# Scan levels on 32x32 quarters, idle products on TensorE, and scattered expert rows in a hybrid encoder layer

## The reference

```
h  = rms_norm(x) * (1 + scale1) + shift1          # scale, shift, gate from silu(c) @ w_ada
p  = h @ w_in                                     # p_rwkv, p_mla, p_gate
y_a = rwkv7_mixer(p_rwkv)                         # 8 heads of 64, forward and backward
y_b = mla_mixer(p_mla)                            # 8 heads, softmax attention
x  = x + gate1 * ((g_a * y_a + g_b * y_b) @ w_out)
x  = x + gate2 * hier_moe(rms_norm(x) * (1 + scale2) + shift2)
```

```
sa    = state @ (-kk_t)
state = state * w_t + outer(sa, kk_t * a_t) + outer(v_t, k_t)
y_t   = state @ r_t
```

## Time and profile before

| | us |
|---|---|
| median of 3 runs | 2738.7 |
| lowest and highest run | 2731.55, 2768.6 |
| the profiled execution | 2732.23 |
| its span in the trace | 2730.4 |

### The profile page before, as it was taken

One profiled execution on the slowest core, in us unless ns is written; L12 is line 12 of the kernel. 1 busy time (PEld: TensorE's weight loads), 2 busy tenths in 40 slices (PEclk: granted clock), 3 DMA queues, 4 the chain that ended last, 5 costly groups with the idle time before them and its releaser, 6 DMA issues. The chain is left out here.

```text
span 2730.4 us, 52710 instructions
## 1 busy us (share of the span) xinstructions
PE 2433.9 (89%) x22191; PEld 1962.5 (72%) x22191; DVE 1595.7 (58%) x2165; ACT 1062.4 (39%) x1865; POOL 677.5 (25%) x498
## 2 busy tenths in 40 slices
PE   5799999999994999999979889998997994999990
PEld 2488887788884999999869756665876883666760
DVE  4444469966652354555445566666886445677756
ACT  5311133344441345445445455554122220555542
POOL 1122245545432345434213320001200000000004
PEclk8899999999995699999869989999998995999995
DMA  8422234443324132332043391103755123999977
GB/s 360 172 77 78 78 106 146 142 158 133 140 110 156 45 88 69 88 92 65 19 133 109 101 326 51 33 24 113 245 164 195 69 70 140 400 422 418 414 298 300
DMA packets 178735, 433.31 MB, mean 159 GB/s; under 512 B 38298, under 2 KB 90298, under 8 KB 160834
## 3 DMA queue, kind: packets, MB, share of 16 engines
q1 hardware_dynamic: 148548, 323.10, 34.1%
q0 software_dynamic: 15840, 57.54, 5.5%
q10 hardware_dynamic: 14112, 49.29, 4.5%
HBM read 307.15 MB, written 122.73 MB: 157 GB/s over the span
## 5 line engine op out<-in xcount | busy, mean ns | idle before, releaser
L99 PE MATMUL ps_in<-h_t_low,w_in_high 128*128 128x512 f32 x960 | 379.6, 395 | 10.5 <-POOL w_in_low L490 10.5
L100 PE MATMUL ps_in<-h_t_high,w_in_low 128*128 128x512 f32 x960 | 374.6, 390 | 0.0
L101 PE MATMUL ps_in<-h_t_high,w_in_high 128*128 128x512 f32 x960 | 374.6, 390 | 0.0
L99 PEld LDWEIGHTS ps_in<-h_t_low,w_in_high 128*128 128x128 f32 x960 | 180.7, 188 | 53.0 <-POOL w_in_low L490 11.5
L1191 POOL TENSOR_TENSOR wkv_levels<-wkv_nt,level_mask 128x1024 f32<-128x1024 f32 x60 | 140.1, 2353 | 274.5 <-ACT wkv_nt L1140 274.5
L101 PEld LDWEIGHTS ps_in<-h_t_high,w_in_high 128*128 128x128 f32 x960 | 180.6, 188 | 38.2
L100 PEld LDWEIGHTS ps_in<-h_t_high,w_in_low 128*128 128x128 f32 x960 | 180.8, 188 | 36.0
L2963 DVE TENSOR_TENSOR w_low<-w_now,w_high 128x2048 fp32r<-128x2048 f32 x64 | 146.7, 2292 | 39.3 <-ACT w_high L2800 39.3
L598 ACT COPY p_row<-ps_in 128x512 f32<-128x512 f32 x72 | 42.3, 588 | 304.5 <-PE ps_in L101 278.9
L2670 POOL DMA_INDIRECT xb<-h,row_ids x34 | 32.9, 967 | 511.1 <-PE ps_xy L2715 285.4
L488 POOL CAST w_in_high<-w_in_tile 128x1024 fp32r<-128x1024 f32 x40 | 46.6, 1164 | 335.8 <-PE ps_in L101 299.5
(11 more groups left out here) (383 smaller groups left out, 5788.9 us busy)
## 6 DMA issues: line engine op xcount, KB each, us to landing
w_now<-in_w SPq DMA_DIRECT2D x68, 1024.0 KB, 9.5
w_tile<-in_w SPq DMA_DIRECT2D x34, 1024.0 KB, 9.4
w_ada_tile<-in_w_ada SPq DMA_DIRECT2D x12, 2048.0 KB, 12.3
wkv_in<-wkv_out SPq DMA_DIRECT2D x24, 1024.0 KB, 3.9
w_in_tile<-in_w_in SPq DMA_DIRECT2D x40, 512.0 KB, 3.6
yb<-yb_tile ACTq DMA_DIRECT2D x34, 512.0 KB, 9.3
yb<-att_zeros POOLq DMA_DIRECT2D x32, 512.0 KB, 18.2
p_t<-p_mixed ACTq DMA_DIRECT2D x24, 512.0 KB, 2.7
```

The costliest lines, as they stand in the source:

```text
L99: nc.tensor.matmul(out, w[0], x[1], start=start, stop=False)
L100: nc.tensor.matmul(out, w[1], x[0], start=False, stop=False)
L101: return nc.tensor.matmul(out, w[0], x[0], start=False, stop=stop)
```

## The change

- In the scan, `nt`, `lev` and `z` hold only the diagonal 32x32 blocks. A level product becomes 64 calls with a 32x32 stationary tile, over four quarters, where it was 32 calls of 64x64. The masks, POOL's multiplications and ACT's copy of z are half as wide (one copy for z), `first_inverse` is one POOL instruction where it was two, `keep_nt` is four copies of 32 partitions where it was two of 64. `half_product` reads `lbm` and not `nt`.
- `keep_busy` issues products that nobody reads: 20 at the start of the scan, 24 before the first level of j = -1, 3 behind each of nine steps of j = -1, 12 at the start of `finish_and_merge`, and in routing 10 behind the counts and 6 behind the product of the lists.
- The product of the lists now gives the place of each row (token + 1536 k + 1; 0 where there is no token). DVE makes two lists from it, `row_from` and `row_to`, with indices beyond the bounds for rows without a token; six DVE instructions where there was one. Gathers and stores skip such rows. `xb` is cleared once.
- The results are stored by POOL as a scatter to `yb`, now laid out as two result rows per token, in place of ACT's direct stores. The zeroing of `yb` is dropped.
- `combine` reads `yb` with one direct transfer per tile, issued by SP; the two loads of `gate2` move from SP's queue to POOL's.

The diff, cut to its core:

```diff
+def keep_busy(nc, consts, out, n):
+    for _ in range(n):
+        nc.tensor.matmul(out, consts["ident"][:], consts["p_end"][:].rearrange("p d f n -> p (d f n)"), start=True, stop=True)
...
-        nt = s.sb("wkv_nt", [P, 2, 2 * H, CH])
-        lev = s.sb("wkv_levels", [P, LEVELS, 2 * H, CH])
+        nt = s.sb("wkv_nt", [P, 2, 2 * H, BLK])
+        lev = s.sb("wkv_levels", [P, LEVELS, 2 * H, BLK])
...
+        quads = [quad(c, b) for c in range(2) for b in range(2)]
...
                 for h in range(2 * H):
-                    for c in range(2):
-                        mm = nc.tensor.matmul(LV[half(c), 0, h], lev[half(c), l, h], x[half(c), i % 2, h], start=True, stop=True)
+                    for a in quads:
+                        mm = nc.tensor.matmul(LV[a, 0, h], lev[a, l, h], x[a, i % 2, h], start=True, stop=True)
...
-                        mm = nc.tensor.matmul(LV[half(c), 1, h], z[half(c), h], xt[half(c), i % 2, h], start=True, stop=True)
+                        mm = nc.tensor.matmul(LV[a, 1, h], z[a, h], xt[a, i % 2, h], start=True, stop=True)
...
+            def idle(j, n):
+                if j < 0:
+                    keep_busy(nc, consts, W[:].rearrange("p h t -> p (h t)")[:, 0:2 * RF * TOK // CH], n)
+            idle(-2, 20)
             for j in range(-2, N):
                 if inner:
+                    idle(j, 24)
                     level_z(j + 1, 1)
+                    idle(j, 3)
...
-                nc.scalar.mul(z[:, :, 0:BLK], LV[:, 0], blk[:, 0:1])
-                nc.scalar.mul(z[:, :, BLK:CH], LV[:, 0], blk[:, 1:2]).then_inc(m["z_kept"], 1)
+                nc.scalar.copy(z[:], LV[:, 0]).then_inc(m["z_kept"], 1)
...
-            for n in range(TOK * TOP // MB, BLOCKS):
-                pool.dma_start(dram["yb"][n], zeros[:]).then_inc(zeros_stored, 16)
...
+            keep_busy(nc, consts, ps_b[:].rearrange("p f t -> p (f t)")[:, 0:2 * RF * TOK // CH], 12)
             for u in range(len(units)):
...
+            def gather(b, offset):
+                pool.indirect_dma_start(out=xb[:, b], out_offset=None, in_=dram["h2"], in_offset=rows_at(offset),
+                                        bounds_check=TOK - 1, oob_is_err=False).then_inc(x_in[b], 16)
+            def scatter(b, offset):
+                pool.indirect_dma_start(out=dram["yb"], out_offset=rows_at(offset), in_=yb[:, b], in_offset=None,
+                                        bounds_check=TOP * TOK - 1, oob_is_err=False).then_inc(stored[b], 16)
+            def store(t):
+                pool.wait_ge(m["y_act"], t + 1)
+                pool.wait_ge(m["y_dve"], t + 1)
+                scatter(t % 2, row_to[:, t:t + 1])
+            for t in range(STATIC + 4):
+                if t < STATIC:
+                    if t >= 2:
+                        pool.wait_ge(m["turned"], t - 1)
+                    gather(t % 2, row_from[:, t:t + 1])
+                if t >= 4:
+                    store(t - 4)
...
+            keep_busy(10)
             for k in range(TOP):
...
+            keep_busy(6)
...
-                act.dma_start(dram["yb"][bass.ds(at, 1)].rearrange("a p d -> p (a d)"), yb[:, b]).then_inc(stored[b], 16)
...
+            def load(t):
+                sp.dma_start(picked[:, b], yb[P * t:P * t + P]).then_inc(gathered[b], 16)
```

More of the change, by code:

```diff
@@ L2597, in route_and_experts @@
         ended, block_e = view("ended", OVER, E), view("block_e", OVER + 1)
-        rank, expert, shift, full, row, blk, dest = (view(n, KT) for n in ("rank", "expert", "shift", "full", "row", "blk", "dest"))
+        rank, expert, shift, full, row, blk = (view(n, KT) for n in ("rank", "expert", "shift", "full", "row", "blk"))
         full_c = view("full_all", KT, TT - 1)
+        place, place_part = (view(n, BLOCKS) for n in ("place", "place_part"))
         early.close()
@@ L2666, in _ @@
         def _(pool):
+            nc.gpsimd.memset(xb[:], 0.0).then_inc(m["cleared"], 1)
+            pool.wait_ge(m["cleared"], 1)
             pool.wait_ge(m["ids"], 1)
-            def gather(t, b, offset):
-                pool.indirect_dma_start(out=xb[:, b], out_offset=None, in_=dram["h2"],
-                                        in_offset=bass.IndirectOffsetOnAxis(ap=offset.bitcast(U32), axis=0)).then_inc(x_in[b], 16)
-            for t in range(STATIC):
-                if t >= 2:
-                    pool.wait_ge(m["turned"], t - 1)
-                gather(t, t % 2, ids[:, t:t + 1])
+            rows_at = lambda offset: bass.IndirectOffsetOnAxis(ap=offset.bitcast(U32), axis=0)
+            def gather(b, offset):
[15 more added lines that the diff above has]
+                    store(t - 4)
             def body(i, ts):
@@ L2696, in _, with keep_busy @@
             nc.tensor.matmul(counts, consts["ones"][:], sums[:, T], start=True, stop=True).then_inc(m["counted"], 1)
+            def keep_busy(n):
+                for _ in range(n):
+                    nc.tensor.matmul(ps_xy[0][:, 0, 0:NTABLES], consts["ident"][:], consts["tables"][:], start=True, stop=True)
+            keep_busy(10)
             for k in range(TOP):
@@ L3005, in _, with combine @@
             over_pairs(dve, body)
-def combine(nc, dram, consts, x1, weight, slot):
+def combine(nc, dram, consts, x1, weight):
     BUF = 4
@@ L3020, in combine @@
         block = ctx.enter_context(nc.Block())
-        yb = dram["yb"].rearrange("b p d -> (b p) d")
+        yb = dram["yb"].rearrange("(k n) d -> n k d", k=TOP)
         @block.sync
         def _(sp):
-            for q in range(2):
-                row = (GATE2 * 2 + q) * DF
-                sp.dma_start(gate2[:, q], dram["mod_rows"][row:row + DF, :].rearrange("f p -> (f p)").partition_broadcast(P)).then_inc(consts_in, 16)
+            def load(t):
+                b = t % BUF
+                if t >= BUF:
+                    sp.wait_ge(done[b], t // BUF)
+                sp.dma_start(picked[:, b], yb[P * t:P * t + P]).then_inc(gathered[b], 16)
+            for t in range(BUF):
+                load(t)
             for t in range(TT):
@@ L3036, in _ @@
         def _(pool):
-            for t in range(TT):
-                b = t % BUF
-                if t >= BUF:
-                    pool.wait_ge(done[b], t // BUF)
-                for k in range(TOP):
-                    pool.indirect_dma_start(out=picked[:, b, k], out_offset=None, in_=yb,
-                                            in_offset=bass.IndirectOffsetOnAxis(ap=slot[:, k, t:t + 1], axis=0)).then_inc(gathered[b], 16)
+            for q in range(2):
+                row = (GATE2 * 2 + q) * DF
+                pool.dma_start(gate2[:, q], dram["mod_rows"][row:row + DF, :].rearrange("f p -> (f p)").partition_broadcast(P)).then_inc(consts_in, 16)
         @block.scalar
@@ L3099, in encoder @@
         weight = s.sb("weight", [P, TOP, TT])
-        slot = s.sb("slot", [P, TOP, TT], U32)
-        route_and_experts(nc, dram, consts, logits, weight, slot)
-        combine(nc, dram, consts, merged, weight, slot)
+        route_and_experts(nc, dram, consts, logits, weight)
+        combine(nc, dram, consts, merged, weight)
 INTERNAL = {
@@ L3116 @@
     "h2": (TOK, D),
-    "yb": (BLOCKS, MB, D),
+    "yb": (TOP * TOK, D),
 }
@@ L3198, in more_layouts @@
     j, t = np.arange(P)[:, None] % CH, np.arange(CH)[None]
-    out["level_mask"] = np.array([((j >> l) ^ (t >> l)) == 1 for l in range(LEVELS)], np.float32).transpose(1, 0, 2).copy()
+    out["level_mask"] = np.array([((j >> l) ^ (t >> l)) == 1 for l in range(LEVELS)], np.float32).transpose(1, 0, 2)
+    out["level_mask"] = np.ascontiguousarray(out["level_mask"].reshape(P, LEVELS, -1, BLK).sum(2))
     out["ident_blocks"] = np.tile(np.eye(BLK, dtype=np.float32), (P // BLK, 1))
```

90 lines of the change are left out of this document (48 added, 42 removed).

## The result

The changed kernel takes 2856.6 us (median of 4 runs, 2842.0 to 2866.4) against 2740.2 (4 runs) for the kernel before: ratio 1.041, 95% interval 1.033 to 1.049. It is slower, by 116 us where I had forecast 49, and the time lies above my range. The profiled execution is 2857.36 us with a span of 2855.5, 125.1 us over that of before.

The account below looks back on a forecast made before the run. PE's work bounds the scan now; after the change, instruction packets would. Scan +58, merging -1.5, routing -4, experts and combine 0 make +52 us, taken as +49: 2788 us, 1.8% slower, range 2680 to 2845.

Parts of the forecast that it names:

- Rivals 1 and 2: Scan: packets never late, 34 us iterations, 2647 us, chance 0.18; or packets bind less, 38 us, 2699, chance 0.14.
- rival 3: Scan levels: small instructions 25 ns apart when 128 follow in a row, 49 us per iteration, about 2820, chance 0.03.
- the clock: Scan iteration: longer stops repeat the fall to half clock; nothing to 3 us, 1.5 taken.
- 34 us of work: Scan iteration: quarters save 5.0 us of PE work, so 39.4 becomes 34 us if nothing else binds.
- 11.2 us of stops: Scan iteration: PE standing for late instruction packets, including 2.5 us for packets delayed by operand loads.
- Rival 4: Scan: clock relapses for most of it, iterations about 57 us, +176, 2900 us in all, chance 0.05.
- The mean over an iteration: Scan: 12.2 packets at 3.5 us each give 42.7 us an iteration, above the 34 us of PE's work.
- Loads: Scan iteration: packets ordered during operand loads come later; 0 to 5 us, 2.5 taken.
- Filling: Scan start: first level 3 us earlier; j = -1 with 11.1 packets takes 39 us at full clock, 15.5 less.
- Merging: Merging stage: idle products raise the clock, some 8 split products run faster; 1.5 us less, at least 0.
- Routing: Routing: full clock for the 48 instructions, five more DVE steps costing 1.2 us; 4 us less, between 0 and 6.
- Combine: Experts and combine: last store 2 us later, direct transfer -3 to +3 (-2 taken); about -2 to +2 in sum, nothing.

Follow-up runs that it names:

- the run with pauses: Kernel before, plus six blocks of unread products with pauses behind the scan's last group; products take 22.6 us after 0.32 us pause, 40 us after 0.68; no total given.
- rates: Kernel before, plus five stretches of unread small and wide products behind the scan's last group; packets 3.6 us apart in the quarters-only stretch; no total given.
- quarters_two: Kernel before with two of a group's eight level products (z of levels 2 and 4) on 32x32 quarters; 2766.0 us, ratio 1.010.
- halves_rest: Changed kernel with the level products back on 64x64 halves, matrices, masks and copies as before, all other parts kept; 2715.3 us, ratio 0.990.
- quarters_all: Kernel before with one edit, all level products on 32x32 quarters of the same tiles; 2855.3 us, ratio 1.042.
- best_a: Changed kernel with levels on 64x64 except group 0's on quarters, no idle products in routing, gate2 on SP's queue; 2713.6 us, ratio 0.992.
- head_pairs: Changed kernel with each quarter product taking two heads at once, odd heads' own matrices left out; 2662.7 us in one run.

## Why the prediction was wrong

- **The direction and the mechanism were right.** Packets of 256 instructions no sooner than about 3.5 us (3.6 measured alone), a stop within the groups, the burst 2.4 us before each end, the quarters at 1.3 us: all there. Rivals 1 and 2 (34 and 38 us an iteration) and rival 3 (25 ns each) are out. On the page "Runtime: NRT & Kernel Launch" of the Trainium skill, section "Instruction fetch mechanics", that crossing is mostly hidden: not for 256 instructions that run in 1.4 us.
- **The term that failed: the clock, "nothing to 3 us, I take 1.5" an iteration. It measured 10.4.** That is 89 us over ten iterations, more than the whole miss. The other two terms were a little high: 34 us of work measured 32.5, and 11.2 us of stops measured 9.55. The supply itself was sized well (3.5 us a packet; 3.6 alone, and 3.6 in the filling, where the clock is 1.00 and 10.6 packets take 38.3 us). The terms are not independent: 12.2 packets by 3.6 us are 43.9 us, more than the 42.1 of work and stops, so a PE at full clock would have stood longer than 9.55 us. How much of the 10.4 that would take back, no run shows.
- **The step that led there** was to price the clock by the one relapse in the trace and then not to multiply it. Two windows of the kernel before, an undisturbed iteration and the one with the 1.44 us stop:

```profile
1041.21:1079.38 38.17, 37.74 (x1056) 35.98 (x1049) 20.24 (x39) 19.77 (x38) 17.24 (x10) 1.00 0.30 86
...
1118.27:1159.72 41.45, 39.58 (x1056) 37.63 (x1048) 20.35 (x39) 19.77 (x38) 17.25 (x10) 0.96 0.29 80
```

  The second is 3.3 us longer: 1.4 of stop and 1.8 of half clock. The changed kernel has some 7 stops an iteration, and 7 times 1.8 is 13 us. That this comes near 10.4 is in part luck: the clock falls only 2.5 times an iteration, but stays down for 9 us on average, where it stayed down for 3.4 in the row above. I excused my 1.5 with "a slower PE also gives the packets time". It does, but the work itself takes longer too: the 64x128 products above 2.08 us instead of 1.1.
- **Rival 4** (57 us, chance 0.05) I argued down with stops "under 1 us". The ten iterations have 69 stops over 0.25 us, 37 of them over 1 us; they reach 4.1 us and have a mean of 1.4, and the run with pauses shows that 0.68 can be enough. The result, 52.4 us, lies between the forecast and rival 4, and the range stopped short of it.
- **The mean over an iteration** (12.2 packets by 3.5 us against 34 us of work) hides where the stops come from. At most two packets are ever ready (rates: 1.5 run before the first stop), so a stretch of long instructions saves up next to nothing for one of short instructions: quarters_two is under the mean limit and is 29 us slower by the median.
- **Loads:** forecast 2.5 us, measured 4.4 with their share of the clock, inside 0 to 5.
- **Filling:** first level 3.8 us earlier (3 forecast), group 0's levels 38.3 us (39; the 11.1 packets were a slip, the trace has 10.6). Last iteration 43.9 (41.5). The idle products are about half of this gain: in halves_rest, with them but without the quarters and POOL's narrower work, the first level comes 0.6 us earlier and group 0's levels take 44.8 us instead of 54.4.
- **A sum of rival 3:** 96 us less the 5 of the filling give 2830, not 2820. It changes no chance.
- **Merging:** the idle products raised merging's first products to full clock, but PE then waits 4.09 us for DVE where it had waited 2.71: 0.3 us gained, not 1.5. Later in the stage 3 us were lost; quarters_all, without that edit, loses 1, and the cause stays open.
- **Routing:** 0 instead of -4. Windows of the changed kernel behind the counts: the 10 idle products once the clock has risen, the wait, and the 48 instructions of the lists:

```profile
2403.50:2409.60 6.10, 6.10 (x17) 2.86 (x16) 5.65 (x14) 0.00 (x0) 0.00 (x0) 1.00 0.00 0
2409.60:2412.34 2.74, 0.15 (x2) 0.01 (x1) 2.59 (x3) 0.00 (x0) 0.00 (x0) 1.00 0.00 0
...
2413.80:2421.60 7.80, 7.80 (x38) 7.80 (x38) 1.99 (x2) 0.00 (x0) 0.00 (x0) 0.50 0.00 0
```

  The idle products do raise the clock, but they end 2.6 us before DVE's tables are there, and at 2413.7 the clock falls again. The 48 instructions take 9.28 us, where I had expected under 7 and they took 10.49; five more DVE steps take that 1.2 us back.
- **Combine:** +4.4 instead of nothing. The store from POOL is 0.8 us later, SP's first load comes 12.2 us behind it instead of 8.8, and DVE waits for `gate_broadcast` (with its loads on SP's queue, in best_a, 3.0 us of this go):

```profile
2783.34 0.98 POOL L2689 DMA_INDIRECT yb<-yb_tile,row_to  x1 [3.69 <-DVE yb_tile L3023]
2795.49 2.10 SPq L3074 DMA_DIRECT2D picked<-yb  x4
...
2806.83 1.28 DVE L3109 SCALAR_TENSOR_TENSOR mixed<-picked,weight,mixed 128x1024 f32<-128x1024 f32 x1 [24.33 <-DMA gate_broadcast<-mod_rows]
```

## What to carry to other kernels

Count instructions as well as busy time before splitting a matrix product: look where 256 of PE's instructions would run in under 3.6 us, place by place and not on average. Where PE will then stand for 0.68 us or more (the shortest pause that lowered the clock here), price the half clock behind it by the work that follows, not by the stop, and count the stops. Idle products pay where PE waits anyway ahead of a busy stretch (the filling, 10 us), if they last until the work comes (in routing they ended 2.6 us early). Small tiles pay where the count doesn't grow (head_pairs), or in a short stretch at full clock (group 0's levels, 4.8 us).

## What I had not expected of the hardware

- After a pause of 0.68 us the clock stays at 0.50 for 39 us of unbroken 64x64 products of 32 columns, and instructions of 128x128 by 192 columns bring it back within some 8 us; after 0.32 us it stays at 1.00.
- In the scan not every stop of 1.5 to 2 us is followed by a fall (after the 1.73 us at 902.12 the clock stayed 1.00, after the 2.87 at 918.57 it fell). What decides there stays open; a fall is not owed to every stop over 0.68 us.
- A product of 128x128 by 192 columns (two instructions) between 32x32 products takes 0.52 us, behind its like 0.35.
